# Who forms the fourth weight difference: VectorE or GpSimd

## The reference, cut to what matters

```python
x = x + token_mix(rmsnorm(x, norm_mix_w[l]), w_in[l], ..., w_out[l])
x = x + cross_attend(rmsnorm(x, norm_xa_w[l]), rmsnorm(mem, norm_mem_w[l]), w_xq[l], w_xkv[l], w_xo[l])
x = x + moe(rmsnorm(x, norm_moe_w[l]), w_router[l], ..., w_gate_up[l], w_down[l], ...)
```

## Time and profile before

| | |
|---|---|
| median of 3 runs | 1188.64 us (1188.61 to 1191.11) |
| profiled execution | 1188.46 us, span of its instructions 1186.7 us |
| granted TensorE clock, mean | 0.987 |
| TensorE, VectorE, ScalarE, GpSimd busy | 1137.7, 379.4, 175.2, 19.0 us |
| chain that ended last | TensorE 68%, DMA 30%, VectorE 1% |
| memory read | 443.20 MB, 374 GB/s over the span |

### The profile page before, as it was taken

One profiled execution on the slowest core, in us unless ns is written; L12 is line 12 of the kernel. 1 busy time (PEld: TensorE's weight loads), 2 busy tenths in 40 slices (PEclk: granted clock), 3 DMA queues, 4 the chain that ended last, 5 costly groups with the idle time before them and its releaser, 6 DMA issues.

```text
span 1186.7 us, 18637 instructions
## 1 busy us (share of the span) xinstructions
PE 1137.7 (96%) x7483; PEld 572.1 (48%) x7484; DVE 379.4 (32%) x896; ACT 175.2 (15%) x366; POOL 19.0 (2%) x58
## 2 busy tenths in 40 slices
PE   9999999999999999999999999999999999999997
PEld 5988879855443443334333333333333333333332
DVE  4688878545222111122212121111111111111112
ACT  5311421243100000001000000000000000000002
POOL 3000010000000000000000000000000000000000
PEclk9999999999999999999999999999999999999999
DMA  9954203989999999999999999999999999999995
GB/s 306 380 196 144 73 10 120 350 334 383 420 426 434 430 429 432 426 436 429 435 430 430 435 428 436 430 434 430 433 432 429 436 428 436 429 434 423 426 424 222
DMA packets 42853, 444.89 MB, mean 375 GB/s; under 512 B 6308, under 2 KB 6772, under 8 KB 26040
## 3 DMA queue, kind: packets, MB, share of 16 engines
q1 hardware_dynamic: 41912, 441.63, 88.9%
q0 software_dynamic: 480, 1.85, 0.7%
q10 hardware_dynamic: 416, 0.79, 0.2%
HBM read 443.20 MB, written 1.05 MB: 374 GB/s over the span
## 4 chain that ended last, share of the span: by engine, by line
PE 68%; DMA 30%; DVE 1%; ACT 0%; SPq 0%; issue 0%; DVEq 0%; ACTq 0%
DMA ring<-in_w_gate_up 30%; PE bank L1168 23%; PE bank L1159 13%; PE bank L733 7%; PE bank L729 4%; PE bank L1198 4%; PE bank L1213 3%; PE bank L712 2%; PE bank L873 1%; PE bank L1095 1%; PE bank L1284 1%; PE bank L1189 1%; PE bank L1275 1%; PE bank L1007 1%; PE bank L1129 1%; PE bank L1087 1%
## 5 line engine op out<-in xcount | busy, mean ns | idle before, releaser
L1168 PE MATMUL bank<-ring,region 128*64 128x512 f32 x2048 | 464.2, 608 | 36.4 <-DMA ring<-in_w_gate_up 36.4
L1168 PEld LDWEIGHTS bank<-ring,region 128*64 128x64 f32 x2048 | 147.1, 140 | 333.9 <-issue 268.6
L1159 PE MATMUL bank<-ring,region 128*64 128x512 f32 x1024 | 226.8, 596 | 0.3 <-ACT region L1407 0.3
L2290 DVE TENSOR_SCALAR region<-bank 128x512 f32<-128x512 f32 x32 | 22.1, 692 | 570.4 <-PE bank L1168 570.4
L1159 PEld LDWEIGHTS bank<-ring,region 128*64 128x64 f32 x1024 | 71.2, 137 | 130.0 <-issue 127.2
L1407 ACT ACTIVATE region<-bank 128x256 f32<-128x256 f32 (+1 forms) x134 | 55.4, 440 | 369.0 <-PE bank L1159 251.0
L733 PE MATMUL bank<-ring 128*128 128x256 f32 x392 | 86.6, 381 | 0.0
L1407 ACT ACTIVATE bank<-region 128x512 f32<-128x512 f32 x32 | 19.2, 601 | 453.1 <-DVE region L2290 453.1
L733 PEld LDWEIGHTS bank<-ring 128*128 128x128 f32 x392 | 73.9, 190 | 10.9 <-issue 0.7
L1198 PE MATMUL bank<-region 64*128 64x512 f32 x264 | 65.6, 615 | 0.1
L1213 PEld LDWEIGHTS bank<-region,r_levels 128*128 128x128 bf16 x1536 | 61.2, 117 | 1.6 <-issue 1.6
(11 more groups left out here) (300 smaller groups left out, 761.4 us busy)
## 6 DMA issues: line engine op xcount, KB each, us to landing
ring<-in_w_gate_up SPq DMA_DIRECT2D x48, 4096.0 KB, 30.2
ring<-in_w_down SPq DMA_DIRECT2D x24, 4096.0 KB, 37.0
ring<-in_w_gate_up SPq DMA_DIRECT2D x26, 2048.0 KB, 15.2
ring<-in_w_down SPq DMA_DIRECT2D x10, 2048.0 KB, 14.3
ring<-in_w_in SPq DMA_DIRECT2D x6, 2048.0 KB, 17.3
ring<-in_w_gate_up SPq DMA_DIRECT2D x11, 1024.0 KB, 35.7
ring<-in_w_xkv SPq DMA_DIRECT2D x4, 2048.0 KB, 10.9
ring<-in_w_down SPq DMA_DIRECT2D x7, 1024.0 KB, 9.1
```

Source lines behind the costliest of these rows:

```text
L1159: last = pe.matmul(bk[half * ROWS:(half + 1) * ROWS, :], lhs, w[:, half * 512:(half + 1) * 512], start=start, stop=stop, skip_group_check= ...
L1168: last = pe.matmul(rows, lhs, columns[:, half], start=start, stop=stop, skip_group_check=True)
L2290: v.tensor_scalar(g_t, bank_g[:, :], LIMIT, None, ALU.min).then_inc(sem["g_clamped"], 1)
```

## The change

The fourth weight difference of the nine panels goes from VectorE's program to GpSimd's, with the same two waits and the same signal. Seven of them stand in GpSimd's program behind the clearing of the tile and ahead of the wait for the diagonal sums, the two of the query panels behind the loads of the experts' down biases and ahead of the wait for the scores. outa and outb stay on VectorE.

```diff
             pool.memset(s_t[:, :], 0.0).then_inc(sem["s_zeroed"], 1)
 
+            def last_difference(name):
+
+                n = SEVEN.index(name) + 1
+                (b11, b12), (b21, b22) = blocks_of_panel(panel_of_job(name))
+                wait_full(pool, name + "A")
+                pool.wait_ge(sem["t2_ready"], n)
+                pool.tensor_tensor(b21, b21, b11, ALU.subtract).then_inc(sem["t4_ready"], 1)
+
+            for name in SEVEN[:SEVEN.index("outa")]:
+                last_difference(name)
+
             wait_full(pool, "diag")
...
+            for name in ("xqa", "xqb"):
+                last_difference(name)
             wait_full(pool, "sc11")
...
-            def combine_last(name):
-
-                n = SEVEN.index(name) + 1
-                (b11, b12), (b21, b22) = blocks_of_panel(panel_of_job(name))
-                wait_full(dve, name + "A")
-                dve.wait_ge(sem["t2_ready"], n)
-                v.tensor_tensor(b21, b21, b11, ALU.subtract).then_inc(sem["t4_ready"], 1)
...
             differences(0)
-            combine_last("gs")
             differences(1)
...
             decayed(0)
-            combine_last("hi")
             decayed(1)
...
                     differences(n + 2)
-                if panel_now:
-                    combine_last(panel_now)
                 if n in (1, 2):
...
-            combine_last("xv")
             for job in level_jobs(64):
...
-            combine_last("xqa")
             join("xqa")
             combine_weights("xqb")
-            combine_last("xqb")
             join("xqb")
```

## The result

The changed kernel takes 1193.67 us (median of 6 runs, 1193.54 to 1194.55), the kernel before 1188.68 us (6 runs, 1188.32 to 1191.24): a ratio of 1.0036 [1.0025, 1.0048], estimated from all runs (that of the medians is 1.0042). It is slower by about 0.4%; 1192.7 was predicted. The profiled execution took 1193.75 us, its span 1192.0 against 1186.7.

The account below looks back on a forecast made before the run. TensorE was taken to bound the mixing stage, expert weight loads the later stretch. Losses of 3.4 us (hg, gv's 0.8 included) and 0.7 (xv) summed to 4.1, giving 1192.7 us; 8-in-10 range 1188.3 to 1197.5.

Parts of the forecast that it names:

- The bound: Mixing stage: TensorE bounds it, VectorE close behind; a TensorE microsecond lost before 150 us counts as lost at the end.
- The duration: GpSimd's subtraction of 1024 elements per partition: 2.3 us, from a select of 128 f32 elements at 2.24 ns each.
- the window of 3.3 us: Each panel: time from the fourth product's completion to the seventh's start; 2.3 us plus 0.1 us each for wake-up and release fits.
- The second rival: All nine panels: the operation takes 5.4 us, every seventh product waits 2.3 us, 1210; at 3.5 us, 1196 to 1198; chance 0.08.
- The exclusion: GpSimd reads and VectorE instructions with two SBUF inputs exclude each other, VectorE held up to 2.3 us; 1191 to 1196.5, chance 0.68.
- the first rival: VectorE and GpSimd read side by side; hg's L1906 starts by 90.4; not slower, 1188.4 to 1189 us; chance 0.21.
- gv into hg: gv's L1905 starts 1.3 us late, hg's L1981 1.0 us late; TensorE loses 0.8 us at hg's third product.
- hg: GpSimd holds L1906 until 93.5, 3.4 us late; TensorE's scores go from 95.87 to 99.3: 3.4 us, gv's 0.8 included.
- gg: L1906 is just done; L1938 is held 0.6 us, within what the next scores leave.
- xk's own subtraction: In xk VectorE waits about as long as the removed instruction took: nothing lost.
- xv: L2067 holds GpSimd to 143.05, GpSimd runs to 145.35; the seventh product, due 144.7, waits to 145.4: 0.7 us.
- gs, hi, xqa and xqb: Window, VectorE idle time or the next bank's wait absorb the holds in these panels: nothing lost.

Follow-up runs that it names:

- All but hg: Against the kernel before, eight of the nine subtractions go to GpSimd and panel hg's stays on VectorE: 1189.96 us, ratio 1.0015.
- hg alone: Against the kernel before, only panel hg's subtraction goes to GpSimd, the other eight stay on VectorE: 1192.38 us against 1188.41, ratio 1.0027.
- the two experiments that have or remove it: Only hg's subtraction on GpSimd, against the kernel before: 1192.38 us; nine identity matmuls added in TensorE's wait in hg's scores, against the changed kernel: 1192.01 us.
- the kernel with five panels: Against the kernel before, only the subtractions of gs, hi, xk, xqa and xqb go to GpSimd: 1189.53 us, ratio 1.0003.
- hg one instruction later: Against the changed kernel, GpSimd's subtraction in hg waits until both of hg's differences are done: 1191.21 us, ratio 1.0024 to the kernel before.
- the extra reads: Against the kernel before, GpSimd does an extra subtraction of data nobody waits for in six panels, gs to xk: 1194.22 us against 1188.60, ratio 1.0048.

## Why the prediction was right, and where its terms were off

**The bound.** That a microsecond of TensorE lost before 150 us is lost at the end held: 5.75 us late at 196.68, 5.3 at the end.

**The duration.** 2.3 us, taken from the select, against 2.34 to 2.36 us undisturbed; the window of 3.3 us held. The second rival (a long operation) falls: TensorE waited for GpSimd in one panel of nine, 0.33 us in xv. The 0.1 us each for wake-up and release were near: GpSimd began 0.14 us after the instruction it waited for in xk (122.82 to 122.96), TensorE 0.06 us after GpSimd in xv (150.36 to 150.42).

**The exclusion.** Right, and it was the point on which the forecast and the first rival parted: L1919 at 91.04 (L1906 before) took 3.10 us. The start that the rival was to be judged by, 90.4, says less than the duration: a held instruction shows its start early and its wait inside. That the joins read one SBUF tensor holds for four of their five instructions; the fourth (L2012, L2017 after) reads two, but never ran beside a subtraction.

**gv into hg: mis-sized.** 1.0 us late was predicted for the first combination of hg (L1994, L1981 before), with 0.8 us of TensorE lost at the third product. It came at 85.60, not 84.73; less the 0.39 us of the start, 0.48 late, and TensorE lost 0.38. The step that failed is that VectorE's masked copy holds GpSimd to its end: the copy L1961 (two of them from 75.90, to 77.25) kept the subtraction of 76.74 for 0.18 us (2.53 less 2.35), where a hold like that of xv (1.29 us of the 1.43 us that were left of L2067) would have made it 2.7. So GpSimd was done at 79.27, and L1918, begun at 77.05, at 80.08. Of the half microsecond by which the term was too large, 0.28 is GpSimd's earlier end; 0.13 is that L1918 needed only 0.81 us behind it, and 0.14 that idle times took up 0.44 us, not 0.3.

**hg: the mechanism right, the sum 2.65 us (0.38 + 2.27) for 3.4.** The difference is for the most part the smaller carry-over of gv (0.48 for 1.0); 0.13 is that L1919 needed only 0.82 us behind GpSimd. All but hg and hg alone show the two parts.

**What was not foreseen: the clock.** 1.64 us at gg (1.7 in the two experiments that have or remove it). The prediction took a gap of TensorE at its length.

**gg: 0.47 us, felt in xk, where nothing was put.** The prediction let gg's hold of L1938 end "within what the next scores leave". It was held (L1951 at 110.24, 1.43 us for 0.95), and gg's last join L2020 came as much later: before, it ended (L2015, 111.55 and 0.42 us) just ahead of the second product of xk, which needs its bank. That product began 1.86 us after xk's first before (112.19 less 110.33) and 2.24 after (117.26 less 115.02): 0.38 us, of which the bracket shows only the 0.22 behind the modelled end of the first. Most of the rest is that the product behind the wait took 1.85 us to the next one's start, for 1.79. In hg alone, with gg's subtraction on VectorE, the wait is gone. xk's own subtraction cost nothing, as predicted: it held L1918 for 1.13 us, for the 1.22 that VectorE gave up.

**xv: right.** 0.61 us for 0.7, by the way described: L2067 from 146.40, GpSimd held to 148.15, the last product at 150.42. gs, hi, xqa and xqb cost nothing, as predicted (no added lateness in the table at hg's first product or behind xqb; the kernel with five panels).

**The sum.** 5.36 us lost up to 153 us (0.38, 2.27, 1.64, 0.47, 0.61) against 4.1, and 0.39 from the start of the profiled executions, which lies ahead of the change; 0.45 were given back in the expert stage; the cause of that stays open. The predicted 1192.7 is near 1193.67 in part because the terms that were too large (0.75 in hg, 0.09 in xv) and those left out (1.64 and 0.47) have opposite signs.

## What to carry to other kernels

Moving an instruction that reads SBUF to GpSimd does not give VectorE its time while VectorE runs instructions with two SBUF inputs: here it gave up 1.2 us a time and was held, in seven of nine panels, for 0.5 to 2.2 us. So such work belongs where VectorE idles, reads a bank (the join at 53.23, beside gs's subtraction, kept its 0.42 us), or is about to wait for another engine. Look for the hold in durations, not in idle time: compare each instruction's length with its own in the kernel before. And price a gap on TensorE at more than its length when it may touch the clock: 2.3 us of waiting cost another 1.7.

## What the runs showed of the hardware that was not expected

- After a pause of 2.4 us and 0.7 us of work at full clock, the granted clock was 0.51 for 3.3 us (in hg alone, behind 2.3 us, 0.53); pauses of 0.36 and 0.47 us (hg one instruction later), and one of 1.22 with one of 0.93 behind it (the extra reads: 12.32 us for gg), left it alone.
- A masked copy whose mask and data lie in SBUF held GpSimd's subtraction for 0.18 us where 0.51 us of it remained, whereas the product L2067 (two SBUF inputs) held it for 1.29 us (3.64 less 2.35) of the 1.43 us between 146.72 and its end at 148.15.
- Once GpSimd ends, the held instruction needs less than its own time: L1918 ended 0.81 us after the subtraction (80.08 less 79.27) and L1919 0.82 (94.14 less 93.32), not 0.95.
- The hold does not go by the size of what is held: in xqa L1785, an instruction on 128x1 with two SBUF inputs, took 2.10 us beside the subtraction, 0.22 otherwise.
